# Joined stage of a hybrid encoder layer: skip weights first in the queue, values' copies in other tiles, outputs turned earlier

## The reference

```python
# long convolution of two input channels groups (256 channels), by FFT of length 2L
z = (v * x1).astype(jnp.float32)
y = jnp.fft.irfft(jnp.fft.rfft(z, n=2 * L, axis=1) * jnp.fft.rfft(k2, axis=0)[None], n=2 * L, axis=1)[:, :L]
y = y + z * skip.astype(jnp.float32)
return (x0.astype(jnp.float32) * y).astype(u.dtype)

# attention over a neighbourhood of 8 rows of a grid of 16 rows by 64 columns, 4 heads of 64
s = jnp.einsum('brqhd,brikhd->bhrqik', grid(q).astype(f32), k_rows.astype(f32)) * (Dh ** -0.5)
p = jax.nn.softmax(s + bias[None], axis=(-2, -1))
o = jnp.einsum('bhrqik,brikhd->brqhd', p, v_rows.astype(f32))
```

## Time and profile before

| | us |
|---|---|
| median of 3 runs | 2064.91 |
| lowest and highest | 2064.57, 2065.87 |
| the profiled execution, its own time | 2068.68 |
| its span | 2066.9 |
| TensorE busy in the span | 1737.8 (84%) |
| VectorE, ScalarE, GpSimd busy | 1111.6, 845.5, 288.4 |

### The profile page before, as it was taken

One profiled execution on the slowest core, in us unless ns is written; L12 is line 12 of the kernel. 1 busy time (PEld: TensorE's weight loads), 2 busy tenths in 40 slices (PEclk: granted clock), 3 DMA queues, 4 the chain that ended last, 5 costly groups with the idle time before them and its releaser, 6 DMA issues. The chain is left out here.

```text
span 2066.9 us, 47853 instructions
## 1 busy us (share of the span) xinstructions
PE 1737.8 (84%) x20423; PEld 1360.4 (66%) x20423; DVE 1111.6 (54%) x1786; ACT 845.5 (41%) x1228; POOL 288.4 (14%) x371
## 2 busy tenths in 40 slices
PE   5999999869896998989885698059999999999980
PEld 4777777757655888888885477046666666666650
DVE  4568898456753333333335632446565565656546
ACT  4256665212222333333332221046566565655632
POOL 0010000011103223332233000220000000000003
PEclk8999999989997999999997798579999999999995
DMA  5124454241102111111312121639998998999837
GB/s 170 62 93 136 137 147 123 66 158 62 61 1 91 49 55 55 55 30 54 145 65 84 54 73 50 247 132 378 362 381 348 372 371 350 377 363 379 350 143 254
DMA packets 95706, 355.62 MB, mean 172 GB/s; under 512 B 8984, under 2 KB 52295, under 8 KB 80936
## 3 DMA queue, kind: packets, MB, share of 16 engines
q1 hardware_dynamic: 82344, 306.83, 39.8%
q0 software_dynamic: 8576, 29.37, 3.7%
q10 hardware_dynamic: 4608, 16.78, 2.0%
HBM read 294.72 MB, written 56.13 MB: 170 GB/s over the span
## 5 line engine op out<-in xcount | busy, mean ns | idle before, releaser
L2236 DVE TENSOR_TENSOR e_rl<-proj,e_rh 128x1024 fp32r<-128x1024 f32 x256 | 304.9, 1222 | 150.1 <-ACT e_rh L2177 148.8
L2177 ACT ACTIVATE e_rh<-proj 128x1024 fp32r<-128x1024 f32 x256 | 258.6, 1053 | 82.4 <-PEq L1884 50.5
L51 PE MATMUL e_ph<-e_rh,e_xh 128*128 128x512 f32 x512 | 221.5, 433 | 17.1 <-DVE e_rl L2236 14.5
L2163 PE MATMUL e_py<-mix,proj 128*128 128x512 f32 x512 | 225.0, 592 | 0.7 <-issue 0.7
L51 PE MATMUL e_ph<-e_rh,e_xl 128*128 128x512 f32 x512 | 201.8, 394 | 0.0
L51 PE MATMUL e_ph<-e_rl,e_xh 128*128 128x512 f32 x512 | 200.5, 392 | 0.0
L51 PE MATMUL a_b<-a_xh,a_wh 128*128 128x512 f32 x432 | 177.9, 412 | 5.9 <-DVE a_wl L580 3.4
L51 PE MATMUL a_b<-a_xl,a_wh 128*128 128x512 f32 x432 | 170.2, 394 | 0.0
L51 PE MATMUL a_b<-a_xh,a_wl 128*128 128x512 f32 x432 | 170.2, 394 | 0.0
L2163 PEld LDWEIGHTS e_py<-mix,proj 128*128 128x128 f32 x512 | 97.1, 190 | 110.5 <-issue 108.1
L1544 ACT ACTIVATE s_th<-s_thb 128x512 f32<-128x512 f32 x128 | 76.4, 597 | 188.4 <-PE s_thb L1413 188.4
(11 more groups left out here) (352 smaller groups left out, 3260.1 us busy)
## 6 DMA issues: line engine op xcount, KB each, us to landing
proj<-in_moe_w SPq DMA_DIRECT2D x64, 2048.0 KB, 14.5
mix<-in_moe_w SPq DMA_DIRECT2D x32, 2048.0 KB, 8.7
proj<-scan_operands SPq DMA_DIRECT2D x64, 320.0 KB, 4.1
scan_operands<-late SPq DMA_DIRECT2D x64, 256.0 KB, 2.6
expert_rows<-e_yo ACTq DMA_DIRECT2D x32, 512.0 KB, 11.2
proj<-in_w_in SPq DMA_DIRECT2D x27, 512.0 KB, 4.1
proj<-in_x SPq DMA_DIRECT2D x16, 512.0 KB, 6.2
expert_rows<-proj SPq DMA_DIRECT2D x1, 7680.0 KB, 24.8
```

Source lines behind the costliest of these rows:

```text
L51: m = e.matmul(out, lhs[a], rhs[b], start=first and n == 0, stop=last and n == 2)
L2163: m = e.matmul(py[h][:, :], at[:, k, :], w2[j][:, k, h * HALF:(h + 1) * HALF], start=(k == 0), stop=(k == KF - 1))
L2177: e.activation(rh[s % RING][:, :], piece(j, s), ACT.Copy).then_inc(high, 1)
L2236: e.tensor_tensor(rl[s % RING][:, :], piece(j, s), rh[s % RING][:, :].bitcast(F32), ALU.subtract).then_inc(low, 1)
```

## The change

Five edits, all in `mixers`:

1. The DMA of the skip weights is issued first of all, and the band goes ahead of the bias.
2. ScalarE multiplies the signal `zc` by the skip weights, in two activations with a scale, ahead of all its other work; VectorE's two multiplications go. VectorE waits for that (`skipped`) before its first output sum.
3. The copies of the values `vt` move from tiles T_K to tiles T_V, and the results `yf` from T_V to T_K. VectorE's wait for `bonus_in` moves from the values' copies to the first write of `yf`. As slices from 8 on lie where the first table of cosines is, VectorE waits for `k_full` before slice 8.
4. TensorE turns the outputs of a row behind its second piece; a third piece comes after them.
5. VectorE keeps the turned outputs before `transform`.

```diff
-        yf = [quad(tile(T_V + i, 1)) for i in range(FH)]
+        yf = [quad(tile(T_K + i, 1)) for i in range(FH)]
...
-        vt = tile(T_K, 4)[:, 0:(ROWS - 1) * NA_D].rearrange("p (s c) -> p s c", c=NA_D)
+        vt = tile(T_V, 4)[:, 0:(ROWS - 1) * NA_D].rearrange("p (s c) -> p s c", c=NA_D)
...
             @block.sync
             def _(e):
+                e.dma_start(skip[:, :], A["hy_skip"]).then_inc(par_in, 16)
                 e.dma_start(cs[0][:, :, :, :, :], A["hy_cs"][0]).then_inc(cs_in[0], 16)
                 e.dma_start(S.mix[:, 2:2 + PAIRS, :], S.proj[:, T_K:T_K + PAIRS, :]).then_inc(bonus_in, 16)
+                e.dma_start(band[:, :], A["na_band"]).then_inc(att_in, 16)
                 e.dma_start(bias[:, :, :, :], A["na_bias"]).then_inc(att_in, 16)
-                e.dma_start(band[:, :], A["na_band"]).then_inc(att_in, 16)
-                e.dma_start(skip[:, :], A["hy_skip"]).then_inc(par_in, 16)
...
-                    for n in range(done + 1, done_by(r)):
-                        piece(n)
-                    done = done_by(r)
+                    piece(done + 1)
                     for p in range(NPAIR):
                         e.wait_ge(o_kept[p], r + 1)
                         e.transpose(f_ps[p], od[p][:, :], S.ident[:, :]).then_inc(f_full[p], 1)
+                    for n in range(done + 2, done_by(r)):
+                        piece(n)
+                    done = done_by(r)
...
                     e.drain()
+                    if i == 0:
+                        e.wait_ge(bonus_in, 16)
                     e.tensor_tensor(yf[i][:, 0, :, :], uv[:, :, 0, :], uv[:, :, 1, :], ALU.add)
...
                     c, o = co // 2, co % 2
+                    if co == 0:
+                        e.wait_ge(skipped, 1)
                     e.wait_ge(y_full, co + 1)
...
-                e.wait_ge(par_in, 16)
-                for c in range(HY_C):
-                    e.tensor_scalar(zc[:, c, :], zc[:, c, :], skip[:, c:c + 1], None, ALU.mult)
-                e.wait_ge(bonus_in, 16)
                 for s in range(0, ROWS - 1):
                     e.wait_ge(v_turned, s + 1)
+                    if s == 8:
+                        e.wait_ge(k_full, 1)
                     e.tensor_copy(vt[:, s, :].rearrange("p (a c) -> p a c", a=NPAIR), t_ps[s % 2][:, 0:NPAIR, :]
...
                     outputs(r)
+                    keep_outputs(r)
                     transform(done_by(r - 1), done_by(r - 2))
-                    keep_outputs(r)
...
+                e.wait_ge(par_in, 16)
+                for c in range(HY_C):
+                    m = e.activation(zc[:, c, :], zc[:, c, :], ACT.Copy, scale=skip[:, c:c + 1])
+                m.then_inc(skipped, 1)
                 odd_sums(PRE, 0)
```

More of the change, by code:

```diff
@@ L827, in mixers @@
         pk, pzf = [pair(t) for t in pf[0:2]], [pair(t) for t in pf[2:4]]
-        par_in = sem("h_par_in")
+        par_in, skipped = sem("h_par_in"), sem("h_skipped")
         cu_in, cs_in, rows_in = ([sem(f"{n}{j}") for j in range(4)] for n in ("h_cu_in", "h_cs_in", "h_rows_in"))
```

## The result

The changed kernel takes 2046.66 us in the median of 4 runs (2044.57 to 2049.58), the kernel before 2064.74 in the same comparison (2063.59 to 2065.87): ratio 0.9917, interval 0.9900 to 0.9934, so 13.6 to 20.6 us less, with the forecast of 15.3 inside. The medians differ by 18.1; the stated range reached from 11.0 to 18.1 less, so the result lies at its very edge. The profiled execution took 2045.08 (span 2043.0).

The account below looks back on a forecast made before the run. TensorE was taken to set the joined stage's pace, apart from a few gaps. Terms -15.7, +1.7, -2.1, -1.8, +1.1, +0.7, +0.8 sum to -15.3, from 2064.91 to 2049.6 us; range 2046.8 to 2053.9.

Parts of the forecast that it names:

- The first gap: Start of the joined stage: TensorE no longer waits 13.5 us for VectorE's first value copy; scores start earlier, -15.7 us.
- What is late next is GpSimd: At the start, GpSimd's bias sums and query copies set the scores at 431.0, not TensorE's own 430.3; otherwise -16.4.
- The covers: Start: ScalarE's multiplications (2.5 us), the cosine table, VectorE's new waits and the reordered band and bias cost nothing.
- Row 0 and the clock: Row 0: outputs wait 1.73 longer with the piece after them, +1.7; the longer gap may drop TensorE's clock, +0.8 (0 to 2.5).
- Rows 3 to 5 and 7 to 9: Keeping outputs before VectorE's sums stops scores of rows 5 and 9 waiting for it: -2.1 and -1.8 us.
- Row 10: Piece 35 waits longer for the last spectrum, as VectorE's sums shift by 1.35: +1.1 us.
- The end: After row 15, one more VectorE output sum falls behind the last keeping, in front of the final products: +0.7 us.
- Other rows of three: Rows 2, 6, 12, 14: turned outputs just fit before the third piece; 0 to 0.2 us each, taken as 0.
- (a): The moved transposition loses: clock falls in row 0, rows 3 to 9 give back half; -10.9, 2054.0 us; chance 0.10.
- (b): The start gains less: bias lands 3 us later, and GpSimd with it; -12.3, 2052.6 us; chance 0.10.
- (c): Slower: turned outputs wait for VectorE in every row of three, 2.1 us each; +1.5, 2066.4 us; chance 0.02.
- (d): At the start, pieces wait for the DMA queue instead of the value copies, so no gain; 2065 us; chance 0.02.

Follow-up runs that it names:

- the multiplying variant: The changed kernel, but VectorE multiplies by the skip weights again ahead of the values' copies, weights still first in the queue: ratio 0.9895, median 2044.05 us.

## Why the prediction was right

The sum of -15.3 stands against -16.7 in the stage and -18.1 in the medians; the 1.4 between the last two lie outside the stage, where traces of one kernel differ by 9. Of the 1.4 by which the stage itself beats the sum, 0.5 came at the start and 1.1 in row 0 with its clock; the rest took 0.2 back. Step by step, from the windows above:

- **The first gap**, -15.7 forecast, -16.2 measured. The strides, the late weights and the free tiles came as worked out: 19.50 from the stage's start to the scores, where the forecast has 19.98. What was mis-sized is GpSimd's part. I took its bias sums at the 4.82 of before, with VectorE's multiplications beside them. Without these they took 4.38 to 4.41 in all nine traces, and the first query copy 0.23 instead of 0.48. In the first trace that let TensorE's own end decide, and the -16.4 that stood as the other end was the nearer one. But "What is late next is GpSimd" holds all the same in all seven other traces with the weights first in the queue: there the scores waited 0.17 to 0.71 for the queries, as TensorE was done earlier or the bias landed later. They began 19.3 to 20.0 after the start. TensorE's own end had a small slip too: the second piece doesn't take as long as the later ones, as I wrote, but 2.02 in the earlier trace rows against 1.89, since the clock rises to full inside it (0.50 granted up to 415.42, 0.76 in the next half microsecond, 1.00 behind that). The Trainium skill (GPSIMD Engine Reference, 1. Specifications) has GpSimd's SBUF interfaces shared with VectorE; the traces agree, and more loudly on the other side, 1.42 against 5.20 us for VectorE's two multiplications.
- **The covers** held: ScalarE's products took 2.19 (2.5 forecast), no piece waited for a table, the new wait before slice 8 never showed. The reordered queue brought the bias 14.1 us after the start in both kernels (424.28 - 410.20, 425.15 - 411.02), and 14.1 to 14.8 after it in the other traces with that queue.
- **Row 0 and the clock**, +1.7 and +0.8 forecast, +1.4 measured. The mechanism is right: VectorE's outputs set the moment and a piece of 1.73 now comes behind them. They came 14.78 after the first scores instead of 15.14, which leaves 1.4. The wait of 2.6 stood in two other traces. But the clock term failed. A clock at half in row 0 was named as the sign that the term is wrong, and it was seen, in piece 8 and not behind the wait, so that it hid inside VectorE's time and cost nothing. In two other traces it fell in or behind the wait, at 2.0 and 3.1 more; in a third, behind a wait of 2.30, it didn't fall. The prediction says nothing of the gaps of 1.75 and 0.65 in front of piece 8, where it fell here.
- **Rows 3 to 5 and 7 to 9**, -2.1 and -1.8 forecast, -2.13 and -1.62 measured, with the predicted waits in place (queries at 2.81 for 3.0, piece 28 at 1.47 for 1.4). That the times fit to 0.2 is luck: both rows of the kernel before move with the clock, and against its second trace row 8 gave back 3.1.
- **Row 10**, +1.1 forecast, +0.91 measured, and a slow clock lasting 0.3 into the next row. **The end**, +0.7 forecast, +0.66 measured. **Other rows of three**: 0, as forecast.

Of the rivals, (a) is refuted as a whole (rows 3 to 9 gave back 3.75 of 3.9, the steady rows paid nothing), though its fallen clock behind row 0's wait did come in two variants; (b) too, the bias landed at most 0.7 later, not 3; (c) and (d) show nowhere. Of the range, the ends that are named give 2047.5 (0.7, 0.8 and 0.6 below the forecast); the last 0.7 down to 2046.8 is worked out nowhere, and the result, 18.1 less, needs it.

## What to carry to other kernels

A first instruction that waits for a tiny transfer costs everything queued behind it: look at what heads each engine's list, at what place in the queue its data has, and at what would be waited for next if that wait were gone. When one producer has two consumers, serve the short one that others wait for first, and choose so row by row: the same new order gained 3.7 us in two rows and lost 3.3 in three others in the first pair of traces, and only windows cut at the rows showed it. Take a second trace of the old kernel before trusting such windows: its total repeated to 0.04 us while one row moved by 1.5. Before moving work to another engine, ask what stood beside it; here the multiplication was dear only next to GpSimd's sums.

## What the runs showed of the hardware

- Two VectorE multiplications of 128x1024 floats by a column took 1.42 us with GpSimd idle and 5.20 beside its two sums of 128x960. The sums took 4.40 without them (VectorE only copied and added results out of PSUM then) and 4.82 beside them. So 3.8 us of the meeting fell on VectorE and 0.4 on GpSimd. It looks like waiting more than like running slowly: GpSimd's sum had started first, and each multiplication (2.59 and 2.69) ended 0.54 behind the sum beside it.
- The granted clock of TensorE fell in or behind gaps of 1.75 and 0.65 in seven of the twelve traces (piece 8 at 2.87 to 3.36, 3.33 in the changed kernel) and not in the other five with the same gaps (1.89, among them the multiplying variant and the kernel before). A term for it can only be a range.
- Whole runs of unchanged code behind the stage differed by 12 us between traces (538.0 to 550.2). Over 400 us of it the granted clock was 1.00 in the two shortest and 0.98 to 0.99 in the two longest.
